# Mixture of experts: weighted expert rows added to the residual in DRAM by an accumulating DMA, and a token gather that leaves out empty slots

## The reference, cut to what matters

```python
ALPHA = (2 * DEPTH) ** 0.25
def moe(x, router_w, router_bias, w_gate, w_up, w_down):
    ...   # sigmoid scores, best group of 4, best 2 experts in it, their scores normed to sum 1: combine (n, 16)
    y = jnp.zeros_like(xt)
    for e in range(N_EXPERTS):            # 16 experts, D_EXPERT = 512
        h = jax.nn.silu(xt @ w_gate[e]) * (xt @ w_up[e])
        y = y + combine[:, e:e + 1] * (h @ w_down[e])
    return y.reshape(shp)

def trunk(...):
    for layer in range(DEPTH):
        ...
        x = layer_norm(ALPHA * x + h, ln_mix_g[layer], ln_mix_b[layer])
        f = moe(x, router_w, router_bias, moe_w_gate[layer], moe_w_up[layer], moe_w_down[layer])
        x = layer_norm(ALPHA * x + f, ln_ffn_g[layer], ln_ffn_b[layer])
```

## Time and profile before

| | |
|---|---|
| median of the runs | 1504.48 us |
| the profiled execution | 1503.68 us, of which the span of the trace is 1501.9 us |
| busy in the span | PE 84%, DVE 66%, ACT 48%, POOL 15% |
| expert loops | about 505 to 808 us and 1148 to 1447 us |
| DMA queues | SP's q1 252.77 MB, POOL's q0 26.22 MB, ACT's q10 16.78 MB |

### The profile page before, as it was taken

One profiled execution on the slowest core, in us unless ns is written; L12 is line 12 of the kernel. 1 busy time (PEld: TensorE's weight loads), 2 busy tenths in 40 slices (PEclk: granted clock), 3 DMA queues, 4 the chain that ended last, 5 costly groups with the idle time before them and its releaser, 6 DMA issues.

```text
span 1501.9 us, 18000 instructions
## 1 busy us (share of the span) xinstructions
PE 1258.5 (84%) x6469; PEld 1011.3 (67%) x6469; DVE 998.2 (66%) x1458; ACT 716.0 (48%) x963; POOL 227.5 (15%) x272
## 2 busy tenths in 40 slices
PE   4999978889998599999994279987995899999940
PEld 4989877775445478888883179943454788888830
DVE  2766354442245599999993932738445999999938
ACT  2533222221012388888872342264122888888822
POOL 3101242211100110000002300136001101000023
PEclk9999989996698699999997589998986999999985
DMA  6120060010525489999963702020444899999733
GB/s 191 57 85 29 1 208 1 1 33 17 172 94 196 158 320 421 410 414 414 408 271 128 226 29 85 1 112 3 175 160 162 318 415 417 414 410 415 288 134 104
DMA packets 63069, 296.59 MB, mean 197 GB/s; under 512 B 6608, under 2 KB 32937, under 8 KB 50720
## 3 DMA queue, kind: packets, MB, share of 16 engines
q1 hardware_dynamic: 51104, 252.77, 43.6%
q0 software_dynamic: 7296, 26.22, 4.9%
q10 hardware_dynamic: 4608, 16.78, 2.8%
HBM read 268.86 MB, written 26.89 MB: 197 GB/s over the span
## 4 chain that ended last, share of the span: by engine, by line
PE 78%; DVE 13%; issue 3%; ACT 3%; POOL 2%; DMA 2%; POOLq 0%; DVEq 0%; ACTq 0%
PE bank L1026 23%; PE bank L1056 12%; PE bank L950 6%; PE bank L612 4%; PE bank L613 4%; PE bank L640 4%; PE bank L641 3%; PE bank L937 3%; PE bank L1016 2%; PE bank L1149 2%; PE bank L961 1%; DVE X L1881 1%; PE bank L599 1%; PE bank L1044 1%; PE bank L836 1%
## 5 line engine op out<-in xcount | busy, mean ns | idle before, releaser
L1174 ACT ACTIVATE GU_HIGH<-work 128x1024 fp32r<-128x1024 f32 x256 | 270.1, 1060 | 64.6 <-PE bank L1026 64.6
L1026 PE MATMUL bank<-GU_HIGH,XGT_HIGH 128*128 128x512 f32 x512 | 205.4, 401 | 13.3 <-DVE XGT_LOW_B L2029 13.3
L2053 DVE TENSOR_TENSOR WUP_LOW<-work,GU_HIGH 128x1024 fp32r<-128x1024 f32 x128 | 153.7, 1222 | 15.2 <-ACT GU_HIGH L1174 10.6
L2053 DVE TENSOR_TENSOR WGT_LOW<-work,GU_HIGH 128x1024 fp32r<-128x1024 f32 x128 | 155.6, 1223 | 12.0 <-ACT GU_HIGH L1174 3.7
L2060 DVE TENSOR_TENSOR WDN_LOW<-work,WDN_HIGH 128x1024 fp32r<-128x1024 f32 x128 | 152.0, 1222 | 8.0 <-ACT WDN_HIGH L1174 3.6
L1174 ACT ACTIVATE WDN_HIGH<-work 128x1024 fp32r<-128x1024 f32 x128 | 135.3, 1062 | 44.1 <-PE bank L1056 44.1
L1174 ACT ACTIVATE work<-bank 128x512 f32<-128x512 f32 (+4 forms) x148 | 59.5, 445 | 132.0 <-PE bank L694 29.6
L1026 PEld LDWEIGHTS bank<-GU_HIGH,XGT_HIGH 128*128 128x128 f32 x512 | 98.4, 192 | 34.1 <-DVE XGT_LOW_B L2029 14.5
L1174 ACT ACTIVATE W_HIGH<-work 128x1024 fp32r<-128x1024 f32 x36 | 38.0, 1057 | 150.7 <-PE bank L613 80.7
L1056 PE MATMUL bank<-WDN_HIGH,HT_HIGH 128*128 128x512 f32 x256 | 103.8, 405 | 2.8 <-DVE HT_LOW L2040 2.8
L1026 PE MATMUL bank<-WGT_LOW,XGT_HIGH 128*128 128x512 f32 x256 | 102.5, 400 | 0.0
(11 more groups left out here) (446 smaller groups left out, 2943.1 us busy)
## 6 DMA issues: line engine op xcount, KB each, us to landing
work<-in_moe_w_gate_dram SPq DMA_DIRECT2D x32, 2048.0 KB
work<-in_moe_w_up_dram SPq DMA_DIRECT2D x32, 2048.0 KB, 10.2
work<-in_moe_w_down_dram SPq DMA_DIRECT2D x32, 2048.0 KB, 9.5
y_rows<-work ACTq DMA_DIRECT2D x32, 512.0 KB
work<-in_ab_w_in_dram SPq DMA_DIRECT2D x10, 1024.0 KB, 5.3
work<-in_c_w_in_dram SPq DMA_DIRECT2D x8, 1024.0 KB, 9.1
x_rows<-X SPq DMA_DIRECT2D x8, 512.0 KB, 2.6
work<-in_c_w_out_dram SPq DMA_DIRECT2D x1, 4096.0 KB, 13.0
```

Source lines behind the costliest of these rows:

```text
L1026: last = mm(psum, x, w, start=(k == m == 0), stop=(k == KD - 1 and m == 2))
L1174: return nc.scalar.activation(out, in_, ACT.Copy, scale=scale)
L2053: V.tensor_tensor(low[u][:, 2 * n:2 * n + 2, :], w[u][:, 2 * n:2 * n + 2, :], high, ALU.subtract)\
```

## The change

The result rows no longer go to slots in DRAM. A new DRAM tensor `x_sum` gets a copy of the normed X before the experts (five stores on SP's queue, after the first two experts' weights). Each expert's result is weighted as it is copied out of PSUM (the weight divided by ALPHA), and POOL adds the 128 rows to `x_sum` with an indirect DMA whose operation is an addition; an empty slot has weight 0 and a row of its own behind the 576 real ones. Adds go one after the other, since two experts can have the same token. After the last add, SP reads `x_sum` back into X, tile by tile, and norm 2 runs on DVE, with only the root on ACT: the statistics (with LN_EPS / ALPHA ** 2, as the sum is smaller by ALPHA), (x - mean) * gain, and times 1/root plus bias. `select_and_bias`, the weighting on ACT, the scaling on ACT and the bias on POOL are gone. The wait of SP ahead of the next mixer's loads for the fourth tile's selected rows is gone as well.

The routing carries three columns of 16 instead of one through the matmuls of L1005: token, weight and a mark of use. From them come, per slot, the token number, the weight and the row to add to; an empty slot's row is at or above 576. The gather of token rows now uses that row list with a bound of 575, so it skips empty slots; both XG buffers are zeroed once per layer ahead of it.

On POOL an expert's add stands ahead of the gather for four experts later. The diff, cut (renamed semaphores, views, constants and `overflow` left out):

```diff
@@ DRAM and SBUF @@
-        slot_list = [nc.dram_tensor(f"slot_list{l}", [SLOTS, 1], I32).ap() for l in range(2)]
-        y_rows = [nc.dram_tensor(f"y_rows{l}", [SLOTS, D], F32).ap() for l in range(2)]
+        slot_list = [nc.dram_tensor(f"slot_list{l}", [SLOTS, 3], I32).ap() for l in range(2)]
+        x_sum = [nc.dram_tensor(f"x_sum{l}", [T + 5 * P, D], F32).ap() for l in range(2)]
...
-        idx_all = sb("idx_all", [P, BLOCKS, NE], I32)
+        idx_all = sb("idx_all", [P, BLOCKS, NE, 3], I32)
...
+        row_cur = sb("row_cur", [P, 2], I32)
+        w_cur = sb("w_cur", [P, 2])
+        w_all = idx_all[:, :, :, :].bitcast(F32)
@@ SP: experts, and new rows_back @@
                 up(l, 1, 1)
                 down(l, 1, 1)
+                for t in range(NT):
+                    sp.dma_start(x_sum[l][P * t:P * t + ROWS[t], :], X[0:ROWS[t], t, :]).then_inc(xsum_out, 16)
...
                 overflow(l)
+                rows_back(l)
...
+            def rows_back(l):
+                for u in range(2):
+                    sp.wait_ge(y_stored[u], arrivals(l, 8))
+                for t in range(NT):
+                    sp.dma_start(X[0:ROWS[t], t, :], x_sum[l][P * t:P * t + ROWS[t], :]).then_inc(x_back[t], 16)
 
             def mixer1():
-                sp.wait_ge(ysel_in[3], 32)
@@ PE: routing @@
-                        last = mm(bank[3][:, 0:NE], holds[:, n, :], tok_of[:, k, NE * t:NE * t + NE],
+                        last = mm(bank[3][:, 0:3 * NE], holds[:, n, :], tok_of[:, k, t, :],
@@ ACT: norm, experts @@
-                weighted(0)
                 for t in range(NT):
-                    if t + 1 < NT:
-                        weighted(t + 1)
                     root(t)
-                    if t:
-                        scaled(t - 1)
-                scaled(NT - 1)
...
-                    copy(YO[u][:, 0:512], bank[7][:, :]).then_inc(y0_out, 1)
-
-                def store(u, g, e):
-                    act.wait_ge(y0_out, g + 1)
-                    act.wait_ge(y1_out, g + 1)
-                    act.dma_start(y_view(l)[0, :, bass.ds(e, 1), :].rearrange("s o d -> s (o d)"), YO[u])\
-                       .then_inc(y_stored[u], 16)
+                    act.wait_ge(w_ready, g + 1)
+                    copy(YO[u][:, 0:512], bank[7][:, :], w_cur[:, u:u + 1]).then_inc(y0_out, 1)
@@ DVE: norm @@
-                        dve.wait_ge(ysel_scaled, l * NT + t + 1)
-                        y1, y2 = Y1[t][0:r, :], Y2[t][0:r, :]
-                        mine(V.scalar_tensor_tensor(y1, y2, wsel[0:r, 1, t:t + 1], y1, ALU.mult, ALU.add))
-                        mine.settle()
-                        last = V.scalar_tensor_tensor(x, x, ALPHA, y1, ALU.mult, ALU.add)
...
+                        dve.wait_ge(x_back[t], 16 * (l + 1))
...
-                    V.tensor_scalar(w[:, 13:14], w[:, 13:14], LN_EPS, None, ALU.add).then_inc(norm_stats, 1)
+                    V.tensor_scalar(w[:, 13:14], w[:, 13:14], LN_EPS / ALPHA ** 2 if q % 2 else LN_EPS, None, ALU.add).then_inc(norm_stats, 1)
...
+                def centred(t):
+                    r = ROWS[t]
+                    x = X[0:r, t, :]
+                    mine(V.scalar_tensor_tensor(x, x, lnw[0:r, t, 12:13], LNP[0:r, 1, 0, :], ALU.subtract, ALU.mult))
+
+                def shifted(t):
+                    r = ROWS[t]
+                    x, w = X[0:r, t, :], lnw[0:r, t, :]
+                    dve.wait_ge(norm_root, q * NT + t + 1)
+                    mine(V.reciprocal(w[:, 14:15], w[:, 14:15]))
+                    mine.settle()
+                    V.scalar_tensor_tensor(x, x, w[:, 14:15], LNP[0:r, 1, 1, :], ALU.mult, ALU.add).then_inc(norm_done, 1)
...
-                dve.wait_ge(xrows_out, 16 * NT * (l + 1))
                 stats(0)
+                centred(0)
                 for t in range(NT):
                     if t + 1 < NT:
                         stats(t + 1)
-                    coefficients(t)
-                    if t:
-                        finish(t - 1)
-                finish(NT - 1)
+                    shifted(t)
+                    if t + 1 < NT:
+                        centred(t + 1)
@@ DVE: route, experts @@
-                    mine(V.tensor_tensor(tok_of[:, k, :].rearrange("p (t e) -> p t e", t=NT), tokens, oh[:, k, :, :],
-                                         ALU.mult))
+                    mine(V.tensor_tensor(tok_of[:, k, :, 0:NE], tokens, oh[:, k, :, :], ALU.mult))
+                    mine(V.tensor_tensor(tok_of[:, k, :, NE:2 * NE], wsel[:, k, :].unsqueeze(2).broadcast_to([P, NT, NE]),
+                                         oh[:, k, :, :], ALU.mult))
+                    mine(V.tensor_copy(tok_of[:, k, :, 2 * NE:3 * NE], oh[:, k, :, :]))
...
-                V.tensor_copy(idx_all[:, 0, :], bank[3][:, 0:NE]).then_inc(idx_ready, 1)
+                V.tensor_copy(idx_all[:, 0, :, 0], bank[3][:, 0:NE]).then_inc(idx_ready, 1)
+                mine(V.tensor_scalar(no_token, bank[3][:, 2 * NE:3 * NE], 1.0, spare_row[:, 0:1], ALU.subtract, ALU.mult))
+                mine(V.tensor_copy(w_all[:, 0, :, 2], bank[3][:, NE:2 * NE]))
+                mine.settle()
+                V.tensor_tensor(idx_all[:, 0, :, 1], bank[3][:, 0:NE], no_token, ALU.subtract).then_inc(idx_ready, 1)
...
-                    V.tensor_copy(YO[u][:, 512:1024], bank[6][:, :]).then_inc(y1_out, 1)
+                    dve.wait_ge(w_ready, g + 1)
+                    V.tensor_scalar(YO[u][:, 512:1024], bank[6][:, :], w_cur[:, u:u + 1], None, ALU.mult).then_inc(y1_out, 1)
@@ POOL: select_and_bias removed, experts @@
                 def gather(u, g, e):
                     at_least(pool, xg_ps, g - 1)
-                    G.tensor_copy(idx_cur[:, u:u + 1], idx_all[:, 0, bass.ds(e, 1)])
+                    G.tensor_copy(idx_cur[:, u:u + 1], idx_all[:, 0, bass.ds(e, 1), 1])
                     pool.drain()
                     pool.indirect_dma_start(
                         out=XG[u], out_offset=None, in_=x_rows[l],
-                        in_offset=bass.IndirectOffsetOnAxis(ap=idx_cur[:, u:u + 1], axis=0)).then_inc(xg_in[u], 16)
+                        in_offset=bass.IndirectOffsetOnAxis(ap=idx_cur[:, u:u + 1], axis=0),
+                        bounds_check=T - 1, oob_is_err=False).then_inc(xg_in[u], 16)
+
+                def weights(u, g, e):
+
+                    at_least(pool, y0_out, g - 1)
+                    at_least(pool, y1_out, g - 1)
+                    G.tensor_copy(w_cur[:, u:u + 1], w_all[:, 0, bass.ds(e, 1), 2]).then_inc(w_ready, 1)
+
+                def add_to_rows(pairs, u, g, e):
+
+                    at_least(pool, y_stored[1 - u], arrivals(l, pairs - 1 + u))
+                    pool.wait_ge(y0_out, g + 1)
+                    pool.wait_ge(y1_out, g + 1)
+                    G.tensor_copy(row_cur[:, u:u + 1], idx_all[:, 0, bass.ds(e, 1), 1])
+                    pool.drain()
+                    pool.indirect_dma_start(
+                        out=x_sum[l], out_offset=bass.IndirectOffsetOnAxis(ap=row_cur[:, u:u + 1], axis=0),
+                        in_=YO[u], in_offset=None, compute_op=ALU.add).then_inc(y_stored[u], 16)
 
                 pool.wait_ge(state_out, 16 * 8)
                 pool.wait_ge(xrows_out, 16 * NT * (l + 1))
-                pool.wait_ge(idx_ready, l + 1)
+                for buf in XG:
+                    do(G.memset(buf, 0.0))
+                pool.wait_ge(idx_ready, 2 * l + 2)
                 gather(0, base, 0)
                 gather(1, base + 1, 1)
-                with pool.Fori(1, NE // 2) as i:
+                for u in range(2):
+                    weights(u, base + u, u)
+                pool.wait_ge(xsum_out, 16 * NT * (l + 1))
+                for u in range(2):
+                    gather(u, base + 2 + u, 2 + u)
+                for u in range(2):
+                    add_to_rows(1, u, base + u, u)
+                    weights(u, base + 2 + u, 2 + u)
+                    gather(u, base + 4 + u, 4 + u)
+                with pool.Fori(3, NE // 2) as i:
                     for u in range(2):
+                        add_to_rows(i - 1, u, i * 2 + (base + u - 4), i * 2 + (u - 4))
+                        weights(u, i * 2 + (base + u - 2), i * 2 + (u - 2))
                         gather(u, i * 2 + (base + u), i * 2 + u)
...
```

More of the change, by code:

```diff
@@ L333, in hybrid_trunk @@
             [sem(f"{n}{u}") for u in range(2)] for n in ("gate_in", "up_in", "down_in", "xg_in", "y_stored"))
-        ysel_in = [sem(f"ysel_in{t}") for t in range(NT)]
+        x_back = [sem(f"x_back{t}") for t in range(NT)]
         xg_ps, xgt_high, xgt_ready, sg_done, h_ready = \
@@ L2377, in experts @@
                         gather(u, i * 2 + (base + u), i * 2 + u)
+                for u in range(2):
+                    add_to_rows(7, u, base + 12 + u, 12 + u)
+                    weights(u, base + 14 + u, 14 + u)
+                for u in range(2):
+                    add_to_rows(8, u, base + 14 + u, 14 + u)
```

(11 more changed lines are left out.)

127 lines of the change are left out of this document (50 added, 77 removed).

## The result

The changed kernel takes 1543.53 us (median of four runs, 1541.2 to 1544.9), the kernel before in the same comparison 1504.57. The ratio is 1.0254, interval 1.0242 to 1.0267: 39 us slower, where the prediction said 13 us faster and gave the range up to 1535.

What follows compares the result with a forecast made beforehand. PE was taken to bound the expert loop, with DVE and DMA engines nearly full. From 1503.7 us, minus 37.2 (ends), plus 3.2 (routing), plus 20.8 (loop) gave 1490.5, with 0.8 to the median 1491; range 1468 to 1535.

Steps and rivals of the forecast that it cites:

- The mechanism: Expert loop: each POOL drain waits until the earlier indirect DMA has landed, the next starting 0.8 us later.
- the round on POOL: Expert loop: POOL's add plus gather, each behind a drain, taken as 19.3 us against 18.4 allowed.
- The ends: End of each layer, last result to end of norm 2: gain of 18.6 us per layer, 37.2 in all.
- The bounds of 34 to 40: Layer ends: range in us of the gain over both layers, from bounds of the add and the read back.
- The routing: Before the first gather: extra small DVE operations and wider matmuls, a loss of 1.6 us per layer, 3.2 in all.
- The loop: Expert loop: PE loses time waiting for gathers that POOL issues late, 10.4 us per layer, 20.8 in all.
- R: POOL's time per expert: landing of add (9.2) plus landing of gather (8.5) plus 1.6 us, taken as 19.3.
- The formula: Expert loop: PE's loss per layer is 12 R - 221.2 us once R exceeds 18.4 us.
- S: Expert loop: time PE loses per layer, forecast 10.4 us; 31 with 9.7 us for both landings.
- Rival 2: Loop: gather stays as long despite empty slots, since the fullest DMA engine sets it; 1508 to 1532 us, chance 0.24.
- Rival 3: Loop: the add occupies DMA engines for three or four times its bytes; 1524 or 1558 us, chance 0.13.
- Rival 1: Loop: shorter landings let POOL's work fit, PE losing under 2 us per layer; 1470, at most 1474 us, chance 0.22.

## Why the prediction was wrong

**The mechanism was right.** The drain holds POOL for the landing, for a DMA that writes to DRAM too; the round on POOL binds; the steps keep 17.75 us at first, and then PE waits ahead of the transposes, not for weights. All of it shows in the profile after, and the run with a semaphore in place of the drains confirms it.

**The ends: right.** 32.3 us were read and 32.0 forecast; the gain was 18.3 and 18.1 for the two layers, against 18.6. Within it the idle landing of the add was 6.1 (5.5 taken, bounds 4.2 and 8.4), the read back to the first statistics 3.9 instead of 3.1, and norm 21.1 instead of 22.3: three small errors that cancel, so the exact hit is luck. The bounds of 34 to 40 were also summed wrongly: with 8.4 us for the add both layers together would gain 31.4.

**The routing: near.** 2.6 + 1.2 = 3.8 us, of which 1.3 was there before the routing began, so 2.5 us against 3.2 forecast.

**The loop: the step that failed is the size of the two landings in R.** The formula holds: the adds from 555.12 to 791.41 are eleven rounds, 236.3 / 11 = 21.5 us, and 12 x 21.5 - 221.2 = 36.8, which is what the first loop lost (36.7). In the second loop R is 21.4, the formula gives 35.2, and 36.8 were lost. But I had put in 19.3, and each 0.1 us of R costs 2.4 us of the time. The error of 2.2 us is 53 us, which is the whole miss: 1491 + 53 = 1544. It has two halves, an add of 10.2 instead of 9.2 and a gather of 9.6 instead of 8.5 (means of the eleven rounds). The landings within the first loop, in this order the gathers before the change, the gathers after it, the adds:

```profile
DMA to landing us min/median/max: 8.3/10.2/11.8
DMA to landing us min/median/max: 6.3/10.1/12.1
DMA to landing us min/median/max: 6.2/9.2/14.7
```

So the first mistake is the 1.2 us that I took off the gather for its empty slots: nothing of it came (10.2 and 10.1; taking all slots again costs 5 us in all). The second: 9.7, the number that I started from, is the median over all gathers, and some of them land in 4 to 6.7 us at the start of a layer, with few weights in flight or none; the loop's own are longer. In the same way the 8.6 and 8.4 over all adds and gathers of the changed kernel are too low for its loop. The third: I let the queue ease as PE falls behind. PE fell behind and the mean busy share went from 1.01 to 0.93, but while most landings ran the engines were still full. The bound that I wrote down, 9.7 us for both, gives R = 21.0 and S = 31, and would have made the forecast 1532.

**The rivals.** Rival 2 was the one that happened, and its point was right: R was above 19.9, and the gather stayed as long as before. Its own price, R 20 to 21 and at most 1532, still fell short. I gave it 0.24 because the one row with 6.5 us spoke for the other side; that was one landing against a median of 9.7 over all. Its reason is true in part: spreading the filled slots gains 12 and 19 us without drains, and 26 with drains where the adds skip, but nothing with drains and full adds, which is this kernel. Rival 3 was nearly true in its size (an add costs the engines 3.2 us, 2.6 times its bytes, where it said three or four times) and false in its weight: with the drains gone, spreading the slots takes back the 12 us that were left (1478.7 against 1466.4), though the adds stay full. Rival 1 came to be once the drains were gone: 1464.5, under its 1470, since the ends gain more there: 30.4 us from the last result to the end of norm 2, with no copy and drain and a shorter landing, which is 20.2 us gained for each.

## What to carry to other kernels

Ahead of an indirect DMA on POOL, wait for the copy of its list by a semaphore, or let it read the list in place, instead of a drain: the drain costs the landing of what is in flight, and a second DMA per step doubles that. Where a loop waits for landings one after the other, sum the means of landings that ran inside the loop, under its load, not a median over all of the kernel, and ask how many microseconds of the end hang on each tenth. And where a transfer skips rows, spread the rows that are left over the partitions of all DMA engines, for in this case the skip saved nothing while the fullest one kept its eight rows.

## What the runs showed of the hardware that I had not expected

- A drain on POOL waits for an indirect DMA to DRAM as for one to SBUF, and ends 0.8 us after the landing; a wait for the copy's semaphore takes 0.28 to 0.77 us.
- An add of 128 rows of 4 KB lands in 6.1 us with idle engines, a plain scatter in 3.3; it takes 3.2 us of the engines' time, of which the addition is 1.7.
- With the skipped slots in partitions 72 to 127, the skipping add lands idle in as much time as the full one (5.7 to 6.3 us). Its last one in the first layer with the spread order (no drains):

```profile
807.44 1.55 POOL L2356 DMA_INDIRECT x_sum<-work,idx_all  x1 [7.42 <-DVE work L2039]
812.33 0.17 POOL L2426 MEMSET work<- 128x3 f32 x3 [3.35 <-DMA x_sum<-work,idx_all]
```

It landed 4.8 us after its issue, which fits an idle landing that is that of the fullest engine, with 5 rows instead of 8.
- A landing depends on what else is on the engines: an add took 6.2 us at a busy share of 0.59 and 12.5 at 1.02, a gather 5.3 at 0.18 and 12.1 at 1.01. Leaving out 56 of 128 rows made the loop's gathers no shorter (median 10.1 us against 10.2).
